# A hybrid decoder step on one core: the samples' depthwise convolution moves from VectorE to GpSimd, beside its gathers

## What is computed

```python
def conv_mix(x, buf, w_pw1, b_pw1, w_dw, b_dw, ln_g, ln_b, w_pw2, b_pw2):
    h = x @ w_pw1 + b_pw1
    u = h[..., :D] * jax.nn.sigmoid(h[..., D:])
    full = jnp.concatenate([buf.astype(u.dtype), u], axis=1)
    c = lax.conv_general_dilated(full, w_dw[:, None, :], window_strides=(1,), padding='VALID',
                                 dimension_numbers=('NWC', 'WIO', 'NWC'), feature_group_count=D) + b_dw
    ...

def peer(...):  # for each token and head
    act = jax.nn.gelu(jnp.einsum('bhkd,bd->bhk', u_tab[idx], xb), approximate=False)
    return jnp.einsum('bhk,bhkd->bd', gate * act, v_tab[idx])
```

## Time and profile before

| | before |
|---|---|
| median of three runs | 3860.83 us |
| profiled execution | 3854.21 us |
| its span | 3852.4 us |
| TensorE matmul, VectorE, ScalarE, GpSimd busy | 74%, 71%, 38%, 37% |
| granted TensorE clock, mean | 0.861 |
| gathers | 1152, 1208.03 MB |
| HBM read | 1303.88 MB, 340 GB/s over the span |

### The profile page before, as it was taken

One profiled execution on the slowest core, in us unless ns is written; L12 is line 12 of the kernel. 1 busy time (PEld: TensorE's weight loads), 2 busy tenths in 40 slices (PEclk: granted clock), 3 DMA queues, 4 the chain that ended last, 5 costly groups with the idle time before them and its releaser, 6 DMA issues.

```text
span 3852.4 us, 56208 instructions
## 1 busy us (share of the span) xinstructions
PE 2855.4 (74%) x20248; PEld 1343.1 (35%) x20248; DVE 2725.7 (71%) x6400; ACT 1449.8 (38%) x4376; POOL 1413.0 (37%) x1272
## 2 busy tenths in 40 slices
PE   5999999686666667788878667798786766666655
PEld 2777767442222212343324213344232222222211
DVE  5566665467666667777787767988776777677775
ACT  1333342134333334444444334444443333333333
POOL 0021111144434444444444444343455444444442
PEclk8999998898888878998889779999898877887877
DMA  2111110399999999999999999999999999999996
GB/s 77 38 29 28 44 32 18 133 425 426 426 427 426 426 426 426 417 393 404 407 426 423 426 425 426 399 374 371 398 416 426 426 425 426 427 426 425 427 427 288
DMA packets 229928, 1313.42 MB, mean 341 GB/s; under 512 B 58768, under 2 KB 61968, under 8 KB 81808
## 3 DMA queue, kind: packets, MB, share of 16 engines
q0 software_dynamic: 165888, 1208.03, 74.9%
q1 hardware_dynamic: 63760, 101.79, 7.5%
HBM read 1303.88 MB, written 5.86 MB: 340 GB/s over the span
## 4 chain that ended last, share of the span: by engine, by line
DMA 38%; PE 19%; DVE 17%; ACT 3%; issue 3%; DVEq 1%; POOL 1%; ACTq 1%; POOLq 0%
DMA arena<-in_uv,arena 37%; DVE arena L1757 9%; PE psum L1329 8%; PE psum L1291 4%; PE psum L1381 3%; PE psum L1411 2%; DVE arena L1846 1%; PE psum L1401 1%; ACT wbuf L1547 1%; POOL arena L1271 1%; ACT arena L1542 1%; DVE arena L1685 1%; PE psum L1340 1%; DVE arena L1682 0%; DVE arena L1820 0%
## 5 line engine op out<-in xcount | busy, mean ns | idle before, releaser
L1329 PE MATMUL psum<-arena,wbuf 64*64 64x512 f32 (+1 forms) x8704 | 1457.0, 742 | 858.0 <-ACT wbuf L1547 832.6
L1271 POOL DMA_INDIRECT arena<-in_uv,arena x1152 | 1333.5, 1158 | 1780.9 <-PE psum L1329 1572.4
L1757 DVE SCALAR_TENSOR_TENSOR arena<-arena 128x1024 f32<-128x1024 f32 x1152 | 1396.3, 1223 | 577.2 <-DMA arena<-in_uv,arena 550.4
L1329 PEld LDWEIGHTS psum<-arena,wbuf 64*64 64x64 f32 (+1 forms) x8704 | 338.2, 155 | 1756.7 <-ACT wbuf L1547 1345.2
L1538 ACT ACTIVATE arena<-arena 128x2 f32<-128x2 f32 x576 | 117.0, 203 | 1663.8 <-DVE arena L1757 1627.9
L1547 ACT ACTIVATE wbuf<-cst,arena 128x64 f32<-128x64 f32 x1152 | 338.2, 340 | 40.8 <-issue 1.4
L1291 PE MATMUL psum<-arena,wbuf 128*128 128x256 f32 (+1 forms) x1024 | 307.0, 447 | 8.6 <-DVE arena L1768 5.8
L1542 ACT ACTIVATE arena<-arena 128x1 f32<-128x1 f32 x1152 | 277.0, 287 | 41.2 <-issue 1.7
L1291 PEld LDWEIGHTS psum<-arena,wbuf 128*128 128x128 f32 x1024 | 199.8, 205 | 168.6 <-issue 127.6
L413 PE MATMUL psum<-arena,wbuf 128*128 128x288 f32 x768 | 216.0, 419 | 10.7 <-DMA wbuf<-in_w_rkv 5.9
L1013 POOL COPY x<-arena 128x256 f32<-128x256 f32 x8 | 3.2, 397 | 430.1 <-DVE x L861 430.1
(11 more groups left out here) (272 smaller groups left out, 3099.9 us busy)
## 6 DMA issues: line engine op xcount, KB each, us to landing
wbuf<-in_w_q SPq DMA_DIRECT2D x64, 576.0 KB
arena<-in_w_pw SPq DMA_DIRECT2D x48, 512.0 KB
arena<-in_uv,arena POOLq DMA_INDIRECT x1152
wbuf<-in_w_rkv SPq DMA_DIRECT2D x24, 512.0 KB, 3.8
wbuf<-in_w_o SPq DMA_DIRECT2D x8, 512.0 KB, 3.6
arena<-in_w_o SPq DMA_DIRECT2D x8, 512.0 KB
x<-in_x SPq DMA_DIRECT2D x1, 2304.0 KB, 8.1
arena<-in_state SPq DMA_DIRECT2D x16, 128.0 KB, 2.9
```

The source lines that it names most:

```text
L1271: pool.indirect_dma_start(ring[:, g % RING, :], None, I["uv"][p // 2], bass.IndirectOffsetOnAxis(ap=idx[:, s % 4, j:j + 1], axis=0)).then_ ...
L1329: last = pe.matmul(ps[e * HD:(e + 1) * HD, 2 * (u % 2) + a if u < NB else 4, :], diag[t, g % DIAGS, :], ring[t, g % RING, D + e * 512:D + ...
L1757: stt(out=row, in0=row, scalar=1.0, in1=tok[p % 2][:, UNITS[p % 2].index(u), :], op0=ALU.mult, op1=ALU.mult, accum_out=dots[:, g % COLS:g ...
```

## The change

The convolution of the samples in half B goes to GpSimd, between its gathers of phase 2. For each chunk it waits for the gated input, makes the products as VectorE did, four for each half, and replaces the reduction by a tree of sums: 15 of the 31 products onto the others, two positions at a time, then 8, 4, 2 and 1 columns for all four positions at once, with a drain between dependent steps. The last operation adds the bias and raises the new semaphore `sampled`. Of the prompt's taps in that half TensorE now makes 10 and VectorE 21; in half A it stays at 16 and 15. SyncE's load of past rows and VectorE's writing of the samples' buffer wait for `sampled` of the chunk two before, and TensorE's `add_up` waits for it too.

```diff
-    PE_TAPS = 16
+    PE_TAPS = (16, 10)
...
+    sampled = K.sem("conv_sampled")
...
                         if c >= 2:
-                            sp.wait_ge(dve_b.sem, dve_b.value(f"{n}.tapped{c - 2}"))
+                            sp.wait_ge(sampled, c - 1)
...
         def _(pool):
+            tick = Tick()
+            HT = ST // 2
+
+            def samples(n, t):
...
+                for c in range(C):
+                    at = t["conv"] + c * t["chunk"] + 1
+                    us = uss[c % 2]
+                    weight = unsq(K.par[:, TAP0:TAP0 + TAPS, c], 1, SB)
+                    bias = K.par[:, B_DW, c:c + 1].unsqueeze(1).to_broadcast([P, HT, SB])
+                    yield from tick.until(at)
+                    pool.wait_ge(dve_b.sem, dve_b.value(f"{n}.glu{c}"))
+                    for e in range(2):
+                        out = cv[1][:, c, 2 * P:WIDTH[1]].rearrange("p (b t) -> p t b", t=ST)
+                        for i in range(HT):
+                            pool.tensor_tensor(prods[:, i], us[:, :, e * HT + i:e * HT + i + TAPS], weight, ALU.mult)
+                            yield from tick.until(at + 4 * e + (i + 1) // 3)
+                        pool.drain()
+                        for i in range(0, HT, 2):
+                            pool.tensor_tensor(prods[:, i:i + 2, :, 0:15], prods[:, i:i + 2, :, 0:15], prods[:, i:i + 2, :, 16:31], ALU.add)
+                        for m in (8, 4, 2):
+                            pool.drain()
+                            yield from tick.until(at + 4 * e + (2 if m == 8 else 3))
+                            pool.tensor_tensor(prods[:, :, :, 0:m], prods[:, :, :, 0:m], prods[:, :, :, m:2 * m], ALU.add)
+                        pool.drain()
+                        pool.tensor_tensor(prods[:, :, :, 0], prods[:, :, :, 0], prods[:, :, :, 1], ALU.add)
+                        pool.drain()
+                        last = pool.tensor_tensor(out[:, e * HT:(e + 1) * HT], prods[:, :, :, 0], bias, ALU.add)
+                        yield from tick.until(at + 4 * e + 4)
+                        pool.drain()
+                    last.then_inc(sampled, 1)
+
...
+                    if p == 2:
+                        tick.now = g - RING - PHASE_ROW[2]
+                        next(work, None)
...
                 def add_up(c):
                     pe.wait_ge(dve_b.sem, dve_b.value(f"{n}.tapped{c}"))
+                    if half:
+                        pe.wait_ge(sampled, c + 1)
...
+                        if c >= 2:
+                            dve.wait_ge(sampled, c - 1)
...
-                    if half:
-                        for e in range(2):
-                            yield from tick.until(at + 1 + 2 * e)
-                            sample_taps(c, us, e)
-                        rest = cv[half][:, c, 2 * P:w]
-                        ts(rest, rest, K.par[:, B_DW, c:c + 1], None, ALU.add)
...
-                    for k in range(PE_TAPS, TAPS):
-                        yield from tick.until(at + 5 + (k - PE_TAPS) * spread // (TAPS - PE_TAPS))
+                    for k in range(PE_TAPS[half], TAPS):
+                        yield from tick.until(at + 5 + (k - PE_TAPS[half]) * spread // (TAPS - PE_TAPS[half]))
```

More of the change, by code:

```diff
@@ L1086, in retrieval_and_conv @@
     dots, gelu, coef = R.cut(COLS), R.cut(COLS), R.cut(COLS)
-    tap_diags = R.cut(PE_TAPS, HD)
+    tap_diags = R.cut(max(PE_TAPS), HD)
     spare = R.cut(1)
@@ L1264, in _ @@
         def _(pool):
+            tick = Tick()
[27 more added lines that the diff above has]
+                    last.then_inc(sampled, 1)
             pool.memset(spare, 0.0).then_inc(row_done, RING)
+            work = samples("cB", times(2))
             for s, (p, head, u) in enumerate(SEQ):
@@ L1273, in _ @@
                                             ).then_inc(here[g % RING], 16)
+                    if p == 2:
+                        tick.now = g - RING - PHASE_ROW[2]
+                        next(work, None)
+                if s + 1 == len(SEQ) or SEQ[s + 1][0] == 3:
+                    tick.now = 10 ** 6
+                    for _ in work:
+                        pass
         @block.tensor
@@ L1406, in taps @@
                     pe.wait_ge(dve_b.sem, dve_b.value(f"{n}.glu{c}"))
-                    for k in range(PE_TAPS):
+                    for k in range(PE_TAPS[half]):
                         yield from tick.until(at + k // 8)
@@ L1410, in taps @@
                             q = slice(e * HD, e * HD + HD)
-                            last = pe.matmul(part[q], tap_diags[q, k, :], ups[c % 2][q, k:k + 2 * P], start=k == 0, stop=k == PE_TAPS - 1)
+                            last = pe.matmul(part[q], tap_diags[q, k, :], ups[c % 2][q, k:k + 2 * P], start=k == 0, stop=k == PE_TAPS[half] - 1)
                     last.then_inc(pe_b.at(f"{n}.tapped{c}"), 1)
@@ L1813, in glu @@
                         dve.drain()
[L1815 to L1824, removed]
                 if half == 0:
```

## The result

The changed kernel takes 4161.94 us in the median of four runs (4160.06 to 4167.34), against 3859.81 us for the kernel before beside it: a ratio of 1.0789, 95% interval 1.0777 to 1.0802. It is 302 us slower. The forecast was 3857 us, no change. The profiled execution took 4167.34 us, its span is 4165.5.

A forecast was written before the change was run, and what follows sets the result against it. The prediction took gathers keeping the DMA engines full as the bound, with VectorE pacing the stage: -28.9 + 28 = -1 us. A shorter TensorE burst won 4 us of 12.7 idle DMA, giving 3857 us, range 3846 to 3887.

The forecast's parts named there:

- the drains: On GpSimd, 14 a chunk, 112 in all: taken at 0.1 us each, 11 us, ends 0 and 34 us.
- all four rivals: Whole-kernel alternatives: 3848 us (chance 0.32), 3893 (0.23), 3896 (0.08), and an empty trade at 3860 (inside the 0.37 case).
- GpSimd's work: 176 added products and sums on GpSimd in the samples' stage: 97 us, products at 0.75 us each.
- rival B: GpSimd issues gathers late and becomes the stage's bound, needing 357 us for 324.5: +32 us, 3893 us; chance 0.23.
- The 92% of load: GpSimd's predicted load in the stage: 299 of 324.5 us, bunched in 8 of 13 rows.
- The shared reads: VectorE and GpSimd meeting at SBUF: VectorE waits 0.25 us for each of 112 GpSimd operations, 28 us.
- Rival C: VectorE stands for each whole GpSimd operation, 0.7 us for each of 112: +35 us, 3896 us; chance 0.08.
- my own case: Likeliest outcome for the whole kernel: about no change, 3857 us, between 3853 and 3868; chance 0.37.
- The relief: VectorE loses the samples (55.8 us) and gains 48 taps (26.9 us) in the stage: net -28.9 us.
- Rival A: GpSimd's reads cost VectorE next to nothing, so all 12.7 us of the stage's idle DMA return: 3848 us; chance 0.32.
- Hidden as long as GpSimd is less than 15 us late: TensorE's sum over chunks waits for GpSimd, due 5 rows, 15 us, earlier; no cost if GpSimd is less late.
- The other two signs of late gathers: In the stage, GpSimd busy beyond 300 us, and its wait for TensorE, 188.6 us before, near nothing.

The follow-up runs named there:

- e2_drains_only: The kernel before with only the change's 112 GpSimd drains added, at the same places: 4101.59 us, ratio 1.0621.
- e6_writes_only: e1_links with every GpSimd operation a memset, a wait for the operation before ahead of each, and the samples' convolution left out: 3852.28 us, ratio 0.9987.
- e1_links: The changed kernel with every GpSimd drain replaced by a wait on the semaphore that the operation before it raises: 3905.12 us, ratio 1.0117.
- e3_relief_only: The changed kernel without the samples' convolution or drains, GpSimd making one 32-column operation per half: 3849.99 us, ratio 0.9972.
- e5_drains_bunched: The changed kernel with each half's eleven GpSimd operations and their drains in one piece between two gathers: 3993.84 us, ratio 1.0354.
- e10_waits_for_landing: The changed kernel with each drain replaced by waits for the operation before and for the newest gather's landing: 4144.27 us, ratio 1.0743.
- e12_links_each: e1_links with a wait for the operation before also ahead of each GpSimd product and first sum: 3884.89 us, ratio 1.0070.
- e8_before_packed_weights: The kernel before, with ScalarE copying a chunk's 31 weights side by side for VectorE's products of the samples: 3853.86 us, ratio 0.9987.
- e9_links_packed_weights: e1_links with ScalarE copying the chunk's 31 weights side by side and GpSimd reading the copy: 3882.24 us, ratio 1.0060.

## Why the prediction was wrong

**The step that failed is the drains.** It read "GpSimd gets 14 a chunk, 112, and no row prices one; I take 0.1 us, 11 us (ends 0 and the 0.30 of a gather's wait, 34 us)." The price of 0.1 us fits a drain that stands behind no gather (0.05 us). What a drain waits for was never asked: the gathers are issued on the same engine, and a drain behind one waits until it has landed. 64 of the 112 stand behind a gather. There GpSimd stood about 330 us in the change where 11 were planned, and the drains alone cost 242 us of time (e2_drains_only). The upper end of 34 us was taken from a row that has nothing to do with a drain. The earlier trace rows held the hint: the kernel lives from a queue of gathers under way, so anything on their engine that might wait for them had to be a rival with the price of a landing, and the gather pieces of 14 to 26 us in the chain of before would have given that price. The last one ahead of the stage:

```profile
2366.29 23.05 DMA arena<-in_uv,arena
```

There was no such rival, and all four rivals lie under 3900.

**GpSimd's work.** The products were taken at 0.75 us with a high end of 0.84; they take 0.81 at least in the change and 0.84 in the median. That GpSimd issues late for its own work (rival B) is refuted: e6_writes_only keeps it nearly as busy and loses nothing, and in e1_links GpSimd is busy 245 of 368 us and waits 108.6 us for TensorE. The 92% of load, from which B was argued, was of no consequence.

**The shared reads.** The mechanism was right and the size was not. The term was 112 x 0.25 = 28 us; in e1_links VectorE lost 67. The 0.25 came from a place where a copy had one input and the operations alternated. Where GpSimd's products stand back to back, VectorE waits for several at once. Rival C (78 us, the full block of each) was nearer than my own case: e1_links lies 45 us above the kernel before, C said 35. The rule of the Trainium skill ("SBUF — State Buffer", section Who interferes with whom) cited there, that the second to issue fully blocks, fits in kind the tap of 2.59 us that starts behind a product. The runs add that this tap stood through three products in a row.

In the changed kernel itself the loss is near the 28 us of the term, by luck. Its lines from 2400 to 3050:

```profile
L1801 DVE SCALAR_TENSOR_TENSOR arena<-arena 128x1024 f32<-128x1024 f32 x109 | 142.6, 1313 | 186.4 <-DMA arena<-in_uv,arena 181.9
L1875 DVE SCALAR_TENSOR_TENSOR arena<-arena,par 128x256 f32<-128x256 f32 x168 | 98.4, 586 | 118.0 <-ACT arena L1647 92.9 <-issue 16.6
```

109 x 0.089 + 168 x 0.102 = 27 us. There the drains spread the stage over some 600 us, and VectorE waits 181.9 of them for data; that its operations meet GpSimd's less often for it is argued, not tried. Without the drains the loss is 67.

**The relief.** VectorE's 28.9 us net: 28.4 in e3_relief_only (257.8 us busy for 286.2). Rival A's gain of 12.7 us: measured alone, 10 us. This part of the reading, that VectorE paces the stage and that at most the idle DMA can be won, stands.

**The waits.** "Hidden as long as GpSimd is less than 15 us late": it was later, and TensorE waited 282.6 us for it. The condition was right. It is a consequence of the drains, since without them (e1_links) no wait of the stage names a GpSimd operation.

**By signs.** The text said it would be wrong if TensorE waited for the samples' semaphore, and that DMA below 0.95 would show late gathers. Both came, the DMA share at 0.56, for a reason that it did not have. The other two signs of late gathers did not come: GpSimd was busy 251 us of 650 and still waited 50.1 us for TensorE.

## What to carry to other kernels

Where GpSimd issues gathers, a drain of GpSimd is a wait for them. Order its own operations by semaphores. Count a drain behind a gather at what is left of that gather's time to its landing, and the queue behind it as emptied. Before moving work to GpSimd beside a VectorE at nearly 90%, price its reads as time in which VectorE's two-input operations stand, and keep its operations from standing back to back. Its memsets cost VectorE 2 us in the whole stage.

## What the runs showed of the hardware that was not expected

- A drain on GpSimd took 0.05 us with no gather since the last drain and 6 to 13 us (medians) behind one (e2_drains_only). It ended 0.2 to 0.4 us behind the landing of the last gather wherever the trace of e5_drains_bunched has both. A wait for the landing in its place gives the same time within 18 us (e10_waits_for_landing).
- Beside GpSimd's products and sums VectorE's taps took 811 ns in the mean (e1_links) in place of 484 (e3_relief_only), and 723 where each waits for the one before (e12_links_each). Memsets with the same waits left the dots at 1224 ns and the taps at 496 (e6_writes_only).
- Three GpSimd products in a row held one tap of VectorE for 2.59 us and were not slowed themselves (e1_links). With a wait between them three taps and three products beside each other took about 0.9 us each (e12_links_each, at 2504).
- A weight read with a step of 8 elements costs VectorE 0.195 us in a product of 248 columns (605 before, 410 in e8_before_packed_weights) and GpSimd 0.16 (824 in e1_links, 665 in e9_links_packed_weights, at the least).
